# Two language-model blocks in fp32 on one core: the turning of the attention weights, two late norms, S5 sums on another engine, and the order of the RWKV preparation changed

## The reference

```
y = concat([rms(y_ssm, ssm_out_norm_w), rms(y_mla, mla_out_norm_w)])
h = h + y @ w_out
h = h + conv_ffn(rms(h))
```

## Time and profile before

| | us |
|---|---|
| median of 3 runs | 3262.21 |
| profiled execution | 3260.85 |
| its span | 3258.3 |
| PE busy | 2999.6 (92%) |
| VectorE busy | 2159.4 (66%) |
| ScalarE busy | 1560.1 (48%) |
| GpSimd busy | 661.4 (20%) |

### The profile page before, as it was taken

How to read it: one execution, slowest core, us unless ns; L and a number is a source line. 1 busy time by engine, 2 the same in 40 slices (tenths; PEclk the granted TensorE clock), 3 DMA queues, 4 the chain that set the end, 5 groups by cost and what they waited for, 6 DMA issues and landing times.

```text
span 3258.3 us, 49703 instructions
## 1 busy us (share of the span) xinstructions
PE 2999.6 (92%) x19690; PEld 2659.3 (82%) x19690; DVE 2159.4 (66%) x3555; ACT 1560.1 (48%) x2542; POOL 661.4 (20%) x829
## 2 busy tenths in 40 slices
PE   5876899999999997899999999898899999999998
PEld 4864778888888887888888888776788888888887
DVE  8787778775777656766666666665666665566655
ACT  3334455554555544455555555444544444344443
POOL 5234102110112000764444440000100111001100
PEclk8987999999999998999999999998999999999999
DMA  4410445556555554322222223432364555655554
GB/s 180 152 65 23 159 143 185 190 175 192 203 194 188 166 176 162 127 72 85 82 85 84 73 82 101 154 112 78 130 203 172 191 186 174 194 201 192 193 167 144
DMA packets 78804, 475.13 MB, mean 146 GB/s; under 512 B 8113, under 2 KB 11185, under 8 KB 37425
## 3 DMA queue, kind: packets, MB, share of 16 engines
q1 hardware_dynamic: 76480, 459.66, 41.4%
q10 hardware_dynamic: 2096, 12.32, 1.1%
HBM read 465.66 MB, written 6.29 MB: 145 GB/s over the span
## 4 chain that ended last, share of the span: by engine, by line
PE 75%; DVE 14%; ACT 6%; issue 2%; POOL 2%; DMA 1%; DVEq 0%; ACTq 0%; SPq 0%
PE bank L684 35%; PE bank L688 22%; PE bank L686 4%; PE bank L687 4%; DVE m L1165 3%; ACT m L1979 2%; PE bank L700 2%; DVE m L1809 1%; PE bank L977 1%; POOL m L2599 1%; POOL m L2603 1%; PE bank L978 1%; PE bank L865 1%; PE bank L974 1%; PE bank L980 1%
## 5 line engine op out<-in xcount | busy, mean ns | idle before, releaser
L688 PE MATMUL bank<-m,m 128*128 128x256 f32 x6864 | 1939.7, 283 | 0.0
L684 PE MATMUL bank<-m,m 128*128 128x512 f32 x4992 | 1757.3, 396 | 17.1 <-POOL m L2478 10.2
L1165 DVE TENSOR_TENSOR m<-m,m 128x1024 fp32r<-128x1024 f32 (+1 forms) x944 | 1077.1, 1149 | 630.6 <-ACT m L1979 616.5
L688 PEld LDWEIGHTS bank<-m,m 128*128 128x128 f32 x6864 | 1311.5, 191 | 1.6
L1979 ACT ACTIVATE m<-m 128x1024 fp32r<-128x1024 f32 (+1 forms) x944 | 912.5, 979 | 786.0 <-PE bank L688 734.8
L684 PEld LDWEIGHTS bank<-m,m 128*128 128x128 f32 x4992 | 941.0, 189 | 231.1 <-issue 14.6
L686 PE MATMUL bank<-m,m 128*128 128x256 f32 x1872 | 573.7, 306 | 77.7 <-DVE m L1165 68.8
L687 PE MATMUL bank<-m,m 128*128 128x256 f32 x1872 | 541.1, 289 | 0.0
L686 PEld LDWEIGHTS bank<-m,m 128*128 128x128 f32 x1872 | 370.4, 198 | 107.5 <-issue 89.2
L687 PEld LDWEIGHTS bank<-m,m 128*128 128x128 f32 x1872 | 371.1, 198 | 3.3 <-issue 1.9
L2580 POOL TENSOR_TENSOR m<-m,m 128x256 fp32r<-128x256 f32 x44 | 63.4, 1441 | 695.6 <-ACT m L2180 695.6
(11 more groups left out here) (361 smaller groups left out, 3018.0 us busy)
## 6 DMA issues: line engine op xcount, KB each, us to landing
m<-in_w_up SPq DMA_DIRECT2D x88, 1024.0 KB, 4.9
m<-in_w_down SPq DMA_DIRECT2D x128, 704.0 KB, 4.0
m<-in_w_gu SPq DMA_DIRECT2D x88, 1024.0 KB, 4.9
m<-in_w_out SPq DMA_DIRECT2D x48, 1024.0 KB, 5.1
m<-in_w_krv SPq DMA_DIRECT2D x48, 1024.0 KB, 4.9
m<-in_w_xbc SPq DMA_DIRECT2D x24, 1024.0 KB, 4.9
m<-in_w_z SPq DMA_DIRECT2D x16, 1024.0 KB, 4.9
m<-in_w_in SPq DMA_DIRECT2D x14, 1024.0 KB, 5.0
```

What stands on the lines that cost most here:

```text
L684: pe.matmul(bank.rearrange("p (a b) -> p a b", a=2), hi, x, start=kc == L.k0, stop=False)
L688: m = pe.matmul(ps, lo, x[:, 0, :], start=False, stop=last)
L1165: v.tensor_tensor(lo_of(k), raw_of(k)[0], hi_of(k).bitcast(F32), SUB).then_inc(*lo_v(("lo", k)))
```

## The change

- Heads: the mask's result is the negated scores, so the minimum is the exp's bias and L1494 goes; L1499 goes, ACT writes a diagonal of reciprocals (`dg4`), and PE turns and divides by a matmul with it in place of the transpose with the identity.
- Norms: N_mla and N_ssm become late. POOL squares and adds their chunks (`sum_squares`), PE adds one total (`add_total`). `rated` multiplies each tile by the rate and adds it to `h`; L_out and L_out2 become narrow. `o` and v change places in `h`, and x comes back in two transfers.
- y is cut within L_out's loop (ACT and POOL), its last chunk after it.
- S5: the sums L1432 and L1449 move to POOL; the sines' product for the cosine (L1410) of levels 5 and 6 becomes four ACT copies with a scale.
- Setup: the transposes of aB and the matmuls of K0 come earlier in the steps, ACT's tables after its copies of aB.
- RWKV `prep`: ACT's two exponentials in two steps, its square root ahead of the factor of k, VectorE's product a step later, PE's `spread` one step later; one empty step fewer in `after`.

```diff
-                v.wait_ge(*s5_v.last)
-                v.tensor_tensor(wc[:, :, 0, :], wa[:, :, 0, :], wb[:, :, 1, :], ADD).then_inc(*s5_v())
...
+                g.tensor_tensor(wc[:, :, 0, :], wa[:, :, 0, :], wb[:, :, 1, :], ADD).then_inc(*s5_g())
                 g.tensor_tensor(wc[:, :, 1, :], wa[:, :, 1, :], wb[:, :, 0, :], SUB).then_inc(*s5_g(("c1", k)))
...
+                g.wait_ge(*s5_v["b", k])
+                g.wait_ge(*s5_g["c", k])
+                g.tensor_tensor(wa[:, :, 1, :], wb[:, :, 1, :], wc[:, :, 0, :], ADD).then_inc(*s5_g(("st", k)))
```

```diff
@@ head on PE, DVE, ACT
-                    m = pe.transpose(banks[b][:, k * 128:(k + 1) * 128], sa[:, k * 128:(k + 1) * 128], ident)
+                    m = pe.matmul(banks[b][:, k * 128:(k + 1) * 128], sa[:, k * 128:(k + 1) * 128], dg4[i % 4],
+                                  start=True, stop=True)
...
-                v.reciprocal(s4[:, 3:4], s4[:, 2:3]).then_inc(*mla_v())
-                v.wait_ge(*mla_v.last)
-                v.tensor_scalar(sa[:, 0:n], sa[:, 0:n], s4[:, 3:4], None, MUL).then_inc(*mla_v(("p", i)))
+                v.reciprocal(s4[:, 3:4], s4[:, 2:3]).then_inc(*mla_v(("p", i)))
...
+                a.activation(dg4[i % 4], ident, ACT.Copy, scale=s4[:, 3:4]).then_inc(*mla_a(("dg", i)))
@@ POOL, new
+            def sum_squares(sig, N, i):
+                total, sq = total_of(N)
+                g.tensor_tensor(sq if i else total, N.chunks[i], N.chunks[i], MUL).then_inc(*sig())
+                g.wait_ge(*sig.last)
+                if i:
+                    g.tensor_tensor(total, total, sq, ADD).then_inc(*sig(("sum", i)))
...
+            def head(i):
+                for _ in range(5):
+                    yield
+                if i % 2:
+                    g.wait_ge(*mla_a["o", i])
+                    sum_squares(mla_g, N_mla, i // 2)
@@ mla_out on PE, DVE
-                add_squares(N_mla)
+                add_total(N_mla)
...
-                norm(N_mla)
-                v.wait_ge(ld_x2, 16)
-                yield
-                yield from linear(L_out, residual("mla", L_out))
+                for i in range(8):
+                    low(N_mla)(i)
+                yield from rate(N_mla)
+                yield from linear(L_out, rated(N_mla, "mla", L_out))
@@ prep on ACT
+                yield
                 a.wait_ge(*wkv_a.last)
                 a.activation(s3, s3, ACT.Exp, scale=math.exp(-0.5)).then_inc(*wkv_a(("pi", i)))
+                yield
+                a.wait_ge(*wkv_v["rn", i])
+                a.activation(rn[:, :, 0:2], rn[:, :, 0:2], ACT.Sqrt).then_inc(*wkv_a(("rn", i)))
                 yield
...
-                a.wait_ge(*wkv_v["rn", i])
-                a.activation(rn[:, :, 0:2], rn[:, :, 0:2], ACT.Sqrt).then_inc(*wkv_a(("rn", i)))
```

More of the change, by code:

```diff
@@ L437, in program @@
         low_cs, low_sn = alloc(32, 16), alloc(32, 16)
+        dg4 = [alloc(128) for _ in range(4)]
         hn = within(hno, 16, T)
@@ L705, in add_squares, with add_total @@
                     add_square(N, i)
+            def add_total(N):
+                pe.wait_ge(*(mla_g if N is N_mla else glu_g)["sum", 7])
+                pe.matmul(banks[N.bank][:, 0:T], ones, total_of(N)[0], start=True, stop=True).then_inc(
+                    *sum_pe((N.id,)))
             def squares(L, *Ns):
@@ L1267, in done, with rated @@
                     v.tensor_tensor(h[:, t, :], h[:, t, :], bank[:, T:2 * T], ADD).then_inc(*res_v((*n, t)))
+                return done
+            def rated(N, *key):
+                def done(t):
+                    L, n = key[-1], key[:-1]
+                    x = xb3[t % 2]
+                    v.wait_ge(*lin_pe["tile", L.number(t)])
+                    v.wait_ge(*norm_a["rr", N.id])
+                    v.wait_ge(*res_v.last)
+                    v.tensor_tensor(x, banks[L.banks[t % len(L.banks)]][:, 0:T], rl, MUL).then_inc(*res_v())
+                    v.wait_ge(ld_x2[t // 8], 16)
+                    v.wait_ge(*res_v.last)
+                    v.tensor_tensor(h[:, t, :], h[:, t, :], x, ADD).then_inc(*res_v((*n, t)))
                 return done
@@ L1918, in glu @@
                 v.tensor_tensor(y2[:, t, :], y[:, t, :], sqb[t % 2], MUL).then_inc(*glu_v(("y2", t)))
-            run(linear(L_glu, glu))
-            norm(N_ssm, glu_v.last)
-            out = Lag(L_out2, residual("ssm", L_out2), lambda t: None, low(N_ffn))
+            gates = Lag(L_glu, glu, low(N_ssm))
+            run(linear(L_glu, gates))
+            gates.tail()
+            out = Lag(L_out2, rated(N_ssm, "ssm", L_out2), lambda t: None, low(N_ffn))
+            run(rate(N_ssm, glu_v.last))
             run(linear(L_out2, out))
@@ L2033, in s5_ab @@
             def s5_ab():
-                for _ in range(8):
+                for _ in range(5):
                     yield
-                yield from s5_tables(0)
                 for r in range(2):
@@ L2109, in mla_out, with cut_y @@
             def mla_out():
+                a.wait_ge(*mla_pe["o", 15])
+                a.dma_start(h[:, 0:8, :], d["xT"][:, 0:8, :]).then_inc(ld_x2[0], 16)
+                a.wait_ge(*mla_a["o", 15])
                 for i in range(8):
-                    square(N_mla, i, mla_a["o", 2 * i + 1])
-                norm(N_mla)
-                a.wait_ge(*norm_v["x", N_mla.x0 + 7])
+                    high(N_mla, i)
+                a.wait_ge(*norm_v["lo", N_mla.x0 + 7])
                 a.wait_ge(*norm_a.last)
-                a.wait_ge(*mla_pe["o", 15])
-                a.dma_start(h, d["xT"]).then_inc(ld_x2, 16)
-                yield
-                yield from linear(L_out, lambda t: None)
+                a.wait_ge(*mla_g["sum", 7])
+                a.dma_start(h[:, 8:16, :], d["xT"][:, 8:16, :]).then_inc(ld_x2[1], 16)
+                yield from rate(N_mla)
+                def cut_y(t):
+                    if t < 14 and t % 2:
+                        a.wait_ge(*s5_a["y", t // 2])
+                        a.activation(hnr[:, 0, t // 2, :], y[:, t // 2, :], ACT.Copy).then_inc(*glu_a(("yhi", t // 2)))
+                yield from linear(L_out, cut_y)
             def squaring(L, *key):
@@ L2401, in glu, with weighted @@
                     *glu_a(("s", t)))
-            run(linear(L_glu, glu))
-            for i in range(8):
-                square(N_ssm, i, glu_v["y2", i], glu_v["y2", 7])
-            norm(N_ssm)
+            def weighted(t):
+                a.wait_ge(*glu_v["y2", t])
+                high(N_ssm, t)
+            gates = Lag(L_glu, glu, weighted)
+            run(linear(L_glu, gates))
+            gates.tail()
             chunks = squaring(L_out2, (N_ffn,), "ssm")
+            run(rate(N_ssm))
             run(linear(L_out2, chunks))
@@ L2558, in mla, with cut_y @@
                 yield
+            def sum_squares(sig, N, i):
[4 more added lines that the diff above has]
+                    g.tensor_tensor(total, total, sq, ADD).then_inc(*sig(("sum", i)))
+                    g.wait_ge(*sig.last)
+            def head(i):
+                for _ in range(5):
+                    yield
+                if i % 2:
+                    g.wait_ge(*mla_a["o", i])
+                    sum_squares(mla_g, N_mla, i // 2)
+            def cut_y(t):
+                if t < 14 and t % 2:
+                    g.wait_ge(*glu_a["yhi", t // 2])
+                    g.tensor_tensor(hnr[:, 1, t // 2, :], y[:, t // 2, :], hnr[:, 0, t // 2, :].bitcast(F32),
+                                    SUB).then_inc(*glu_g(("ylo", t // 2)))
             def mla_out():
-                norm(N_mla)
                 yield
-                yield from linear(L_out)
+                yield from linear(L_out, cut_y)
             def conv(t):
```

118 lines of the change are left out of this document (65 added, 53 removed).

## The result

The changed kernel takes 3187.81 us (median of 4 runs, 3187.53 to 3192.46) against 3262.57 (4 runs, 3261.06 to 3263.58) beside it: a ratio of 0.9775, 95% interval 0.9758 to 0.9792. The prediction was 3203 in 3180 to 3234. Of the numbers that it gave, that of rival 3 (3186, "more than forecast", chance 0.12) lies nearest.

The account below looks back on a forecast made before the run. TensorE, busy 92% of the span, was taken as the bound, so its waits and low-clock stretches count. Terms 7 - 13.7 - 4.5 - 11.9 - 33 - 2.5 = -58.6 us gave 3203 us, range 3180 to 3234.

Parts of the forecast that it names:

- rival 3: More than forecast: RWKV's waits go whole (-43) and heads stay even, 3186 us; chance 0.12.
- three terms: Attention half of w_out -13.7 us, gate projection -4.5, SSM half of w_out -11.9.
- The 2.5 us for a cold start: Attention half of w_out: 2.5 us added to its new time for a cold start.
- three quarters of 43: RWKV preparation: 29.2 us of waits and seven cold stretches could go, 43; three quarters taken, -33.
- the discount and the bound: RWKV preparation: -33 us after taking three quarters, against the bound of -43.
- Rival 4: RWKV: VectorE asks for the solve's matmuls as PE issues them; eight blocks cost +50, 3287 us; chance 0.04.
- -2.5 and 0: Ahead of the heads: setup three steps earlier for K0 gives -2.5 us; the pairs before the heads give 0.
- the same pairs run with fewer conflicts: 0: S5 pairs before the heads: fewer conflicts but no gain, 0 us, bounds -3 to +4.
- +7: Heads: +1.8 us a batch, +7 for four, bounds -17 to +20.
- Squares stand ahead of the pair's sums: Heads, POOL's program: squares run until about 3.8 us, two sums until 5.7; scans start 2.0 us later.
- rival 2: POOL bounds the heads, busy 66 of 80 us: +20 instead of +7, 3216 us; chance 0.12.

Follow-up runs that it names:

- norms_alone: Kernel before with only the two late norms (narrow w_out, POOL's squares, y cut within w_out's loop, x back in two transfers): 3231.0 us.
- prep_pe_old: Changed kernel with PE asking for ACT's square root in its old step, one step earlier; ACT and VectorE as changed: 3216.7 us.
- tables_back: Changed kernel with the sine product of the cosine's levels 5 and 6 on VectorE again, without ACT's copies: 3194.7 us.
- sums_back: Changed kernel with both S5 sums of a pair on VectorE again: 3188.6 us.
- setup_undone: Changed kernel with the old steps for aB's transposes, K0's matmuls and ACT's tables: 3193.6 us.

## Why the prediction was right, and where its sizes were off

- *w_out and the gate projection*: three terms within 0.7 us each. First block 3.43 us after the last product with v (2.8 forecast, the wait for POOL being 3.08); the attention half 54.88 (55.2 forecast); no wait for x; `norms_alone` gives these gains by itself. The 2.5 us for a cold start within the attention half came from no row; the change loses 0.03 x 54.88 = 1.6 us to the clock there.
- *RWKV preparation*: the mechanism as put (PE's request one step behind ACT's square root), and shown by `prep_pe_old`. The size was taken at three quarters of 43; 37.3 came. The waits for the square root lost 26.3 of their 29.2 us. The gain lies in the last five of the seven stretches from one request to the next: 83.4 us became 76.8, and four of 85.3 became 77.7, while the first two (47.8 and 73.1) became 46.0 and 75.8. Of the 7.6 us of a steady period 3.85 are the wait and 1.9 TensorE's lower clock behind it, as forecast; 1.8 are shorter waits for VectorE at two later matmuls (L946 and L963, 1.3 and 0.9 us, became 0.4 and none), which were no term. So the total came out between the discount and the bound with two errors against each other: too much for the first blocks, too little for the others. Rival 4's price didn't show. That ACT's new order would matter was never a term, and with PE's later request it doesn't.
- *Ahead of the heads*: -2.5 and 0 came as -6.5. At the first scan the change is 2.6 us earlier, the setup's forecast. The rest, 3.9, comes between it and the scores (104.8 us became 100.9), and the step that failed is "the same pairs run with fewer conflicts: 0". `tables_back` gives 4.5 of these back and `sums_back` 0.6, so the tables are the part. `setup_undone` gives back 1.8 of them too, and how that and the tables' 4.5 share the 3.9 stays open.
- *Heads*: +7 came as +2.1, and the reasons held. "Squares stand ahead of the pair's sums" is the true bound of three batches: moving them takes 8.1 us out. The first turning waits for ACT, whose diagonals last 0.39 us each and overlap, so that one costs ACT 0.32 (0.28 forecast), and the turning takes twelve records in 2.93 us (3.2 forecast). Two prices were too large. POOL's moved sums took 0.74 and 0.81 us, not 0.96, and POOL was busy 56 of 82 us where rival 2 had 66 of 80: rival 2 (POOL bounds the heads, +20) had the right engine. And from the fourth turning to the last product with v the change takes 7.4 us, before 9.2, and with the norms alone it is 7.5.
- The Trainium skill (GPSIMD Engine Reference, section 4.1, Engine selection) spoke against moving sums to POOL. The trace agrees on the single operation (0.74 us on POOL against 0.42 on VectorE), and moving them back makes the heads 4.4 us shorter. For the kernel it doesn't decide: with the squares two steps later and the sums on POOL the heads are shorter still, and ahead of the heads, where POOL is busy for 48 of 119 us (100 to 219), the slower engine costs nothing that shows.

The three misses (4.0 us ahead of the heads, 4.9 in them, 4.3 in RWKV) all point the same way and make up 13.2 of the 14.3 us. So the forecast wasn't carried by errors that cancel between the stages, and its number was 15 us too high. Rival 3 (waits go whole, heads even) came within 2 us: the heads were nearly so (+2.1) and the waits went to nine tenths, but its 43 us for RWKV came as 37.3, and the 4.0 us more ahead of the heads, which it hadn't, made up much of that. Its closeness is in part luck.

## What to carry to other kernels

Where one engine asks for a result in the very step in which another makes it, behind a table load, let it ask one step later: that was worth 28.9 us here, and the order within the maker's step nothing once it was done. Work moved to a helper engine is priced by what stands behind it in that engine's order, not by its busy share: 3.2 us of squares at the head of POOL's queue cost 8 us in three batches, and moving them two steps later gave these back. And before a difference of 2 or 3 us between two traces is put down to an edit, look whether it is there already before the first edited instruction runs; here it was, for the moved sums.

## What the runs showed of the hardware

POOL and VectorE instructions take longer beside some of the other's: four scans (L1473) take 1.37 us where POOL stands idle (252.04) and 2.06 beside its sum and sines (261.17); POOL's L2583 takes 1.26 us for 256 elements beside VectorE's table product at 267.85, where its L2580 takes 0.61 beside the mask and the reductions. A level's product on ACT as four copies with a scale costs ACT 1.0 us, and taking it back to VectorE cost 6.9 us in all; why it pays wasn't shown. At a granted clock of 0.50 the turning of a batch takes 2.93 us as twelve records against the diagonals and 2.00 as six with the identity.
